# A third ready product at the change of stages, tile statistics on GpSimd, and the last forms of the third tile pair behind the scale of tile 7

## The reference, cut to what matters

```
h = rms_norm(x, norm_g)                       # x is 2048 tokens x 1024
proj = h @ w_in                               # 1024 -> 5120 columns: u, z_pool, q, k, v, z_attn, gates
y_pool = multiscale_pool(u) * silu(z_pool)    # trailing means over 2, 4, 8, 16 tokens, a map per group
y_attn = stick_breaking(q, k, v) * silu(z_attn)
merged = sigmoid(gate0) * (y_pool @ w_pool_up) + sigmoid(gate1) * (y_attn @ w_attn_up)
out = rms_norm(x + merged @ w_out, final_g)
```

## Time and profile before

| | |
|---|---|
| runs | 1581.51, 1579.95, 1577.16 us; median 1579.95 |
| the profiled execution's own time | 1579.27 us |
| its span | 1577.4 us |
| PE busy | 1530.4 us (97%) |
| DVE, POOL, ACT busy | 1237.2, 1102.0, 856.2 us |
| mean granted clock | 0.992 |

### The profile page before, as it was taken

The page is one execution under the profiler, slowest core; times in us unless marked ns, Lnnn a source line. Parts: engine busy times, 40 slices in busy tenths (PEclk is TensorE's granted clock), DMA queues, the critical chain, the costliest instruction groups (busy, mean ns, idle before and its releaser), DMA issues. The chain is left out here.

```text
span 1577.4 us, 24982 instructions
## 1 busy us (share of the span) xinstructions
PE 1530.4 (97%) x7770; PEld 1275.2 (81%) x7770; DVE 1237.2 (78%) x1592; ACT 856.2 (54%) x1653; POOL 1102.0 (70%) x770
## 2 busy tenths in 40 slices
PE   7999999998999999999998999999999999999998
PEld 5787878886888887888877888888888788888886
DVE  7968595766987788887897887798878656687987
ACT  6546554444666665666665676666766512233342
POOL 4899876985977678777766776787756334456774
PEclk9999999999999999999999999999999999999999
DMA  7468942465344343343694442443423688764552
GB/s 270 151 240 310 376 125 92 118 214 169 87 109 112 89 127 102 94 139 93 185 329 143 129 120 87 120 114 99 121 71 83 209 272 257 251 197 166 181 190 110
DMA packets 170803, 254.45 MB, mean 161 GB/s; under 512 B 48417, under 2 KB 82209, under 8 KB 170674
## 3 DMA queue, kind: packets, MB, share of 16 engines
q1 hardware_dynamic: 170674, 252.85, 51.2%
HBM read 166.80 MB, written 85.99 MB: 160 GB/s over the span
## 5 line engine op out<-in xcount | busy, mean ns | idle before, releaser
L2103 POOL TENSOR_TENSOR ring<-raw,ring 128x512 fp32r<-128x512 f32 x140 | 241.2, 1723 | 154.3 <-ACT ring L1950 143.9
L2045 DVE TENSOR_TENSOR_SCAN left<-keep,left 128x512 f32<-128x512 f32 x192 | 283.8, 1478 | 61.9 <-issue 40.1
L1870 PE MATMUL psum<-hT,ring 128*128 128x512 f32 x664 | 273.9, 412 | 14.7 <-ACT sum_a L1983 5.1
L1874 PE MATMUL psum<-hT,ring 128*128 128x512 f32 x664 | 271.8, 409 | 0.0
L1872 PE MATMUL psum<-hT,ring 128*128 128x512 f32 x664 | 271.2, 408 | 0.0
L1956 ACT ACTIVATE keep<-psum 128x512 f32<-128x512 f32 (+3 forms) x320 | 170.8, 534 | 131.8 <-PE psum L1893 119.2
L1963 ACT ACTIVATE wt<-psum 128x512 fp32r<-128x512 f32 (+3 forms) x320 | 171.0, 534 | 111.3 <-PE psum L1901 108.6
L2051 DVE TENSOR_TENSOR wt<-psum,wt 128x512 fp32r<-128x512 f32 (+3 forms) x320 | 190.3, 595 | 16.5 <-ACT wt L1963 13.9
L1913 PEld LDWEIGHTS psum<-wt,vm 128*128 128x128 f32 x1088 | 171.6, 189 | 26.9 <-DVE wt L2051 1.5
L1913 PE MATMUL psum<-wt,vm 128*128 128x256 f32 x1088 | 181.5, 281 | 1.0 <-DVE wt L2051 1.0
L1901 PE MATMUL psum<-ident,left 128*128 128x128 f32 x1088 | 171.1, 272 | 4.0 <-DVE wt L2051 4.0
(11 more groups left out here) (262 smaller groups left out, 3410.1 us busy)
## 6 DMA issues: line engine op xcount, KB each, us to landing
raw<-in_w_strips SPq DMA_DIRECT2D x144, 256.0 KB, 4.0
qm<-qk_scratch SPq DMA_DIRECT2D x128, 128.0 KB, 4.5
gate<-gate_scratch SPq DMA_DIRECT2D x64, 256.0 KB, 4.7
form_scratch<-hT SPq DMA_DIRECT2D x28, 512.0 KB, 7.0
hT<-form_scratch SPq DMA_DIRECT2D x28, 512.0 KB, 8.3
km<-qk_scratch SPq DMA_DIRECT2D x64, 128.0 KB, 3.7
merged_scratch<-rows SPq DMA_DIRECT2D x32, 256.0 KB, 5.0
mt<-merged_scratch SPq DMA_DIRECT2D x16, 512.0 KB, 5.8
```

The source lines that it names most:

```text
L1870: pe.matmul(o, hi, m_hi, start=k == 0 and not onto, stop=False, skip_group_check=onto)
L1874: last = pe.matmul(o, lo, m_hi, start=False, stop=k == HK - 1, skip_group_check=onto)
L2045: dve.tensor_tensor_scan(left[:, n % LN, span][:, ::-1], k, k, carry, ALU.mult, ALU.bypass).then_inc(scanned, 1)
L2103: pool.tensor_tensor(out_, a, b, op).then_inc(s, 1)
```

## The change

READY_PARTS becomes 3, so the front also makes S2 of stage 3's first group. Its copy of A11 goes to a tile of its own (`ready_sum`), which stage 3 uses as its `sum_a`. The Newton step of batches 2, 3, 4 and 5 moves from DVE to POOL. `tile_high(2)` moves ahead of `root(3)` on ACT, and DVE's `mean` of a batch waits until the batch before is finished. T3 and T4 of the third pair of each half move from the step of tile 6 (14) to behind the scale of tile 7 (15). `pooled_high` moves one slot later and ahead of the splits. Results of groups 5 and 11 come one slot behind their part in place of two. In stage 3, the result of A22 goes to the head of its step on ACT, and its silu ahead of the scan on DVE.

```diff
-READY_PARTS = 2
+READY_PARTS = 3
...
-                   if r is not None and r < FRONT_PARTS and (r == FRONT_PARTS - 1) == last]
+                   if r is not None and r < FRONT_PARTS and (r // FORMS % HALF_GROUPS == HALF_GROUPS - 1) == soon]
...
@@ front, GpSimd
+            def factors(b):
+                tiles = range(*BATCHES[b])
+                pool.wait_ge(rooted, b + 1)
+                for n in tiles:
+                    last = pool.tensor_scalar(stat[:, 4, n:n + 1], stat[:, 3, n:n + 1], stat[:, 3, n:n + 1],
+                                              stat[:, 1, n:n + 1], ALU.mult, ALU.mult)
+                last.then_inc(statistics, 1)
+                pool.wait_ge(statistics, 5 * b + 3)
...
             def tile_step(n):
                 tile_low(n)
                 i = n % FRONT_TILES
+                if n == 2:
+                    factors(4)
+                if batch_at(n) is not None:
+                    factors(batch_at(n))
...
+            factors(2)
             tile_low(1)
+            factors(3)
@@ front, ScalarE
+                if g == FRONT_GROUPS:
+                    act.wait_ge(mixed, 2 * MIXED_FIRST)
+                act.activation(ready_sum if g == FRONT_GROUPS else sum_u if j == S2 else sum_a, bank(g, j), ACT.Copy
...
             make_diag(2)
             square(3)
+            tile_high(2)
             root(3)
             make_diag(3)
             square(4)
...
+                for f, q, step in pooling_at_slot(s):
+                    if step == LEVELS[q] + 2:
+                        pooled_high(f, q)
                 for w in splits_at(s):
                     split_w(w)
                 for g, j in results_at(s):
                     result_high(g, j)
...
-                for f, q, step in pooling_at_slot(s):
-                    if step == LEVELS[q] + 1:
-                        pooled_high(f, q)
@@ front, VectorE
+                if b:
+                    dve.wait_ge(statistics, 5 * b)
                 dve.wait_ge(squared, BATCHES[b][1])
...
             mean(2)
-            factors(2)
             first_forms(0)
             mean(3)
-            factors(3)
             scale(2)
-            mean(4)
-            factors(4)
...
-                    last_forms(n // 2 - 1)
+                    if i < 6:
+                        last_forms(n // 2 - 1)
                     form_low(n // 2 - 1, T1)
...
                 if n is not None:
                     form_low(n // 2, T1)
+                    last_forms(n // 2 - 1)
                     last_forms(n // 2)
@@ stage 3, ScalarE
+            act.sem_inc(taken, 1)
...
-                        if s == PART_END[part(g, j)]:
+                        if s == PART_END[part(g, j)] and part(g, j) > 0:
                             take(g, j)
+                for k in at(RESULT, s):
+                    if k % 4 == 3:
+                        result(k)
                 if 0 <= s < ALL:
                     remaining(s)
@@ stage 3, VectorE
+                for k in at(RESULT, s):
+                    if kind(k // 4) < 2 and k % 4 == 3:
+                        silu(k)
                 if s - AV_LAG - 1 in LAST:
                     add_halves(s - AV_LAG - 1)
                 if s < ALL:
                     scan(s)
```

More of the change, by code:

```diff
@@ L287, in build @@
         last_stores = stage3(nc, sem, psum, Arena(nc, heads.at, mix_at), raws, ring, ident, bcol, v_ends, hT, w_strips, mix_t,
-                             mix_d, yp_d, za_d, at_d, gate_d, form_d, form_in, staging, stored3, y_stored, opening, head_loads)
+                             mix_d, yp_d, za_d, at_d, gate_d, form_d, form_in, staging, stored3, y_stored, opening, head_loads, ready_sum)
         stage4(nc, sem, psum, Arena(nc, w_at + up_bytes, free_at), Arena(nc, hT_at + 2 * BLOCK + up_bytes, w_at),
@@ L318, in front @@
 def front(nc, sem, psum, at, free_at, hT_at, ident, ident_r, gcol, bcol, pscol, v_ends, hT, ring, raws, staging, ring_at, raw1_at,
-          x, x_T, norm_gT, w_v, b_gateT, pool_scaleT, w_strips, pool_w, pool_fix, v_d, qk_d, mix_d, form_d, head_loads):
+          x, x_T, norm_gT, w_v, b_gateT, pool_scaleT, w_strips, pool_w, pool_fix, v_d, qk_d, mix_d, form_d, head_loads, ready_sum):
     G = len(WINDOWS)
@@ L447, in scaled, with raw_of @@
         return x_tile(n)[:, hb * HK:(hb + 1) * HK, :]
+    def raw_of(pair, j):
+        f, i = divmod(pair, HK)
+        return len(RAW_ORDER) * f + RAW_ORDER.index((i, j)) + 1
     def on_vector(pair, j):
@@ L550, in results_at @@
         lagged = [PART_AT.get(s - 2), PART_AT.get(s - 1)]
-        at_slot = [r for r, last in zip(lagged, (False, True))
-                   if r is not None and r < FRONT_PARTS and (r == FRONT_PARTS - 1) == last]
+        at_slot = [r for r, soon in zip(lagged, (False, True))
+                   if r is not None and r < FRONT_PARTS and (r // FORMS % HALF_GROUPS == HALF_GROUPS - 1) == soon]
         return [(r // FORMS, r % FORMS) for r in at_slot if not is_u(r // FORMS) and r % FORMS in OUT_PARTS]
@@ L892, in low_w @@
                     step(at_g[S4][:, :, :], at_g[A12][:, :, :], at_g[S2][:, :, :], ALU.subtract, w_formed, 4 * g + 4)
+            def factors(b):
[6 more added lines that the diff above has]
+                pool.wait_ge(statistics, 5 * b + 3)
+                part = stat[:, 5, tiles.start:tiles.stop]
+                pool.tensor_scalar(part, stat[:, 4, tiles.start:tiles.stop], -0.5, 1.5, ALU.mult, ALU.add).then_inc(statistics, 1)
+                pool.wait_ge(statistics, 5 * b + 4)
+                for n in tiles:
+                    last = pool.tensor_scalar(stat[:, 6, n:n + 1], stat[:, 5, n:n + 1], stat[:, 3, n:n + 1], 1.0,
+                                              ALU.mult, ALU.mult)
+                last.then_inc(statistics, 1)
             def tile_low(n):
@@ L1003, in tile_step @@
                 i = n % FRONT_TILES
-                tile_high(n)
+                if n != 2:
+                    tile_high(n)
                 if later(n):
@@ L1026, in take @@
                     act.wait_ge(summed, 3 * (g - 1) + FRONT_ADD[S3 if j == A11 else S4])
-                act.activation(sum_u if j == S2 else sum_a, bank(g, j), ACT.Copy).then_inc(taken, 1)
+                if g == FRONT_GROUPS:
+                    act.wait_ge(mixed, 2 * MIXED_FIRST)
+                act.activation(ready_sum if g == FRONT_GROUPS else sum_u if j == S2 else sum_a, bank(g, j), ACT.Copy
+                               ).then_inc(taken, 1)
             def close_u(g):
@@ L1094, in _ @@
                 r = PART_AT.get(s - 1)
-                if r is not None and r < FRONT_PARTS:
+                if r is not None and r <= FRONT_PARTS:
                     g, j = divmod(r, FORMS)
@@ L1105, in _ @@
                 if n is not None:
-                    for j in T_ORDER:
+                    for j in (T1, T2):
+                        form_high(n // 2, j)
+                    for j in (T3, T4):
+                        form_high(n // 2 - 1, j)
+                    for j in (T3, T4):
                         form_high(n // 2, j)
                     copy_v(n - 2)
+                for f, q, step in pooling_at_slot(s):
+                    if step == LEVELS[q] + 2:
+                        pooled_high(f, q)
                 for w in splits_at(s):
@@ L1155, in factors @@
                 dve.wait_ge(rooted, b + 1)
-                if tiles.stop - tiles.start <= 2:
+                if tiles.stop - tiles.start == 1:
                     root_of = [stat[:, 3, n:n + 1] for n in range(tiles.start, tiles.stop)]
@@ L1211, in tile_step @@
                 i = n % FRONT_TILES
-                if n != 2:
+                if n == 2:
+                    mean(4)
+                else:
                     scale(n)
@@ L1494, in stage3 @@
 def stage3(nc, sem, psum, sb, raws, ring, ident, bcol, v_ends, hT, w_strips, mix_t, mix_d, yp_d, za_d,
-           at_d, gate_d, form_d, form_in, staging, sum_stored, y_stored, opening, head_loads):
+           at_d, gate_d, form_d, form_in, staging, sum_stored, y_stored, opening, head_loads, sum_a):
     ITEMS = attention_items()
@@ L1654, in stage3 @@
     RESULT = [fin[result_part(k)] + 1 for k in range(RESULTS)]
+    assert all(a < b for a, b in zip(RESULT, RESULT[1:]))
     FORM_STEP = {}
@@ L1673, in stage3 @@
     blocks = [{**raws[i], S1: raws[i][A11], S4: raws[i][A12], S2: second} for i in range(2)]
-    sum_a, sum_b, sum_c, sum_d = (sb(f"sum_{n}", [P, CH])[:, :] for n in "abcd")
+    sum_b, sum_c, sum_d = (sb(f"sum_{n}", [P, CH])[:, :] for n in "bcd")
     res, sum_e = staging[:, 0, :], staging[:, 1, :]
@@ L2020, in _ @@
                 for k in at(RESULT, s):
-                    result(k)
+                    if k % 4 < 3:
+                        result(k)
                 if ALL - 4 <= s < ALL:
@@ L2087, in _ @@
                 for k in at(RESULT, s):
-                    if kind(k // 4) < 2:
+                    if kind(k // 4) < 2 and k % 4 < 3:
                         silu(k)
```

26 lines of the change are left out of this document (13 added, 13 removed).

## The result

The changed kernel is **slower**: 1584.39 us median (19 runs, 1579.04 to 1589.59) against 1578.45 (19 runs) of the kernel before, ratio 1.0035, 95% interval 1.0024 to 1.0047, some 5.5 us or a third of a percent. The forecast was 1573.5, and slower by over 0.3% had been given a chance of 0.07. The execution whose trace is shown took 1587.43 us (span 1585.6); a second trace of the same kernel, told further down, took 1581.44. Runs of one kernel spread by 3 to 14 us, so small differences are read from ratios with their intervals, and from traces only stretch by stretch.

The account below looks back on a forecast made before the run. The prediction took PE, busy 97% of the span, to bound the kernel. Its terms, -2.3 - 5.4 + 1.0 + 1.4 - 0.6 - 1.4 + 1.5 = -5.8, took 1579.27 us to 1573.5, range 1567 to 1580.

Parts of the forecast that it names:

- The third product: Change of stages: S2 fills PE's pause, the clock still falls, 12 full-speed matmuls leave the rest: -2.3 us.
- ACT splits three weights in step 0: Start of stage 3: one more ring place is freed earlier; priced 0, up to 1.5 us if the start runs dry.
- The cover named: Start of stage 3: 24 matmuls in the ring cover the earlier splits and group 1's forms, so price 0.
- The held clock: Rival, change of stages: the clock holds through the shorter pause, giving 1571.0 us; chance 0.23.
- A22's result first: Stage 3: PE's waits for `sum_d` go, -5.4 us; delayed `remaining` and scan add +1.0, between 0 and 5.4.
- changed places: Rival, stage 3: the later scan makes `wt` late by what `sum_d` no longer costs, giving 1577.9 us; chance 0.18.
- The half-way forms: Stage 3: most parts move one step ahead, loads and readers alike; priced 0, with one step (2.6 us) either way.
- The opening: Tiles 2 and 3: Newton steps on POOL, 0.35 us each, put scale 3 at 35.5 and tile 3 later: +1.4 us.
- Tile 7 earlier: First part of the front: scale 7 comes earlier on DVE with `last_forms` behind it, POOL waits less: -0.6 us.
- The moved forms delay T3 and T4 of two pairs: Front: forms made later are first read two parts (5 us) later; price 0.
- `pooled_high`: Front, at 139.54: the copy of S2 goes ahead, PE's 1.37 us wait goes, -1.4; seven other cases 0, up to +1.
- Group 5: Front, tiles 8 and 9: the copy of S2 falls behind ACT's wait for a store: +1.5 us, +2.5 at most.

Follow-up runs that it names:

- run 6: Kernel before with the third ready product alone, S2 of stage 3's first group made ahead of the pause: 1582.51 us, ratio 1.0024.
- run 4: Changed kernel with ACT's splits of weights 7, 8 and 9 in their old steps (1, 2 and 5): 1581.05 us, ratio 1.0009 to the kernel before.
- run 7: Changed kernel, three ready products, but every part of stage 3 in its old step: 1574.41 us, ratio 0.9977 to the kernel before.
- run 9: Changed kernel with loads behind the v stores, Newton steps on DVE, group 5's results and stage 3's parts as before: 1563.78 us, ratio 0.9901.
- the last run of 8: Changed kernel with two ready products, loads behind the v stores, Newton steps on DVE, group 5's results in old slots: 1567.26 us, ratio 0.9922.
- run 5: Kernel before with A22's result first alone, on ACT and DVE in stage 3: 1571.58 us, ratio 0.9954.
- run 8: Changed kernel with two ready products; successively loads behind v stores, Newton steps on DVE, group 5 in old slots: 1571.64, 1568.22, 1567.26 us.
- run 1: Changed kernel with the third pair's T3 and T4 where they were, ACT's high parts in old order: 1582.33 us, ratio 1.0021 to the kernel before.
- run 2: Changed kernel with loads of groups 1 and 7 issued behind the v stores of tiles 4 and 12: 1578.40 us, ratio 0.9994 to the kernel before.
- run 10: Fastest kernel with loads of groups 1 and 7 ahead of the v stores again: 1566.67 us; with the forms also back where they were: 1566.25 us.
- run 3: Changed kernel with two ready products (`READY_PARTS = 2`), all else as changed: 1572.12 us, ratio 0.9960 to the kernel before.

## Why the prediction was wrong

By the trace shown the sum should have been +8.2, it was -5.8. The steps, in the prediction's order:

- **The third product, -2.3.** The change of stages came out as worked out: S1 behind DVE's add, a pause of 3.2 us for 2.9, the clock fallen; score 0 is 1.0 later, for 0.4. The step that failed is the last one of that part, **"ACT splits three weights in step 0 ... I price it 0, with up to 1.5 if the start runs dry"**. It does run dry, by 5.3 us (run 6 has the same, without the rest). About half of that is the split that stands for POOL's form (run 4), the rest DVE, because every part comes one part earlier against the scores. The cover named, 24 matmuls in the ring, feeds PE; what ran dry was the chain of scan, `wt` and weighing, which goes through ACT, POOL and DVE. With every part in its old step the start does not run dry (runs 7, 9), and the same product gains 3.3 us by the ratios (run 9 against the last run of 8).
- **The held clock** was a rival for this one pause. Two traces of one kernel give both cases, and the row taken to decide it (2.75 fell, 1.87 did not) cannot decide it: 3.6 held.
- **A22's result first, -5.4 + 1.0.** The waits went; nothing changed places with them (`wt` 4.0 in four before and in run 5), so +1.0 was not owed. Alone it measures 7.3, with an interval from 4.4 to 9.9, so the term was right in kind and perhaps under-sized. In the trace of run 5 part of the excess lies at the half-way stretch; that it belongs to A22 there and not to the spread between executions is not settled by one trace.
- **The half-way forms, 0 with one step either way.** The scale was right, and the sign is no longer open with A22 first: the stretch takes 80.9 to 85.4 us where the parts come a step early and 76.1 to 80.1 where they do not (run 7).
- **The opening, +1.4.** Sixteen Newton instructions on POOL took 0.36 us each: the 0.35 was right, as a mean. The rule of the Trainium skill that stood beside it (GPSIMD Engine Reference, section 3) has VectorE roughly twice as fast. Line against line the trace agrees roughly: 0.52 on POOL against 0.27 on DVE for the first instruction of a step, 0.26 against 0.21 for the last, 1.6 times over both. The 0.54 worked out by it was too high because 0.27 is the dearest of the three lines on DVE. Still the opening cost 2.75 at tile 2, twice the term. The mean of batch 4 came at 29.8, not 29.1, POOL began that batch at 30.52, when ACT's root was there, and was done with it some 2.2 us later, and scale 3 started at 36.64, not 35.5. PE stood 3.41 us for the diagonal inside tile 2. Undone (run 8), the traces give 2.8 back at tile 2 and 2.1 at the last ready part, and the time falls by 1.9 by the ratios.
- **Tile 7 earlier, -0.6:** -0.4. Right.
- **"The moved forms delay T3 and T4 of two pairs, first read two parts (5 us) later; price 0": the second failed step.** It asked who reads the forms and not who waits for their sources to come free: SP's loads of groups 1 and 7, with the v stores queued behind. The shift grew by 4.6 us in each half by the trace shown, by 5.9 and 2.3 by the second. How much of this reaches the end stays open: four comparisons (runs 1, 2, 8, 10) show 6.8, 7.5, 8.3 and 4.9 us at the last ready part, and 2.2, 6.5, 2.5 and 6.5 in the time by the ratios. In the trace of run 10 part of it is given back at two places where the granted clock did not fall; more is not shown. Nor is it settled why moving the forms back gains less than moving the loads.
- **`pooled_high`, -1.4:** -1.7 in the first trace. Right, and right that the other seven don't matter.
- **Group 5, +1.5:** +1.9 with a fall of the clock (+3.9 up to the first half of tile 8, for +2.5, and 2.0 given back at tile 9, for 1), -0.5 without; undone, 1.6 us less by the ratios, which is within their noise. It was right in place and cause; the size differs between executions.

So the terms that had a price came out within 3 us of it; two effects priced at nothing cost 9 and 5 us in the trace shown. The range missed because it reached to the bounds of the priced terms only. None of the rivals describes it.

## What to carry to other kernels

When an instruction is moved later, list not only the readers of its result but every queue that waits for what it reads to be overwritten, and what is queued behind that wait; here it was cured by issuing the waiting loads behind the first of the stores. When work is pulled into a pause, keep the rest of the schedule in its old steps, or each later producer is asked for its part too early. And price a wait of PE twice, alone and with a fall of the granted clock behind it.

## What the runs showed of the hardware

A fall of PE's granted clock behind a wait does not follow from the length of the wait alone. At S2 of group 6 waits of 2.5 (run 10) and 2.7 us went with a fall, 2.0 (second trace) and 3.0 (run 3) did not; at S2 of group 0 3.6 and 4.1 did, 3.4 (run 10) did not. At the change of stages the same program has a fall behind 3.2 in one execution and none behind 3.6 in another. At S2 of group 6 the shift grew by 0.3 more than the wait without the fall (2.34 for 2.02) and by 1.9 more with it (4.56 for 2.69). This adds to the spread between executions: the two traces of run 4 are 8.3 us apart before stage 3 begins, with waits of 6.1 and 3.7 us in group 5 and at S2 of group 6 together and a granted clock of 0.76 and 1.00 from 186 to 200 us.

Sixteen Newton instructions of one or two columns took POOL 0.19 to 0.98 us each (mean 0.36); the first and the last of a step took 0.52 and 0.26 there, and 0.27 and 0.21 on DVE.
